# Layer 0's input projection on split operands for 18 of 20 tiles, the request part of the 31-tap convolution on GpSimd, and the first taps of the 4-tap convolution on ScalarE

## The reference, cut to what matters

```python
proj = h @ w_in                      # 640 x 1024 times 1024 x 2568
a_val, a_gate, z, xbc, dt_raw = split(proj, ...)     # 512, 512, 512, 1024, 8 columns
a_glu = a_val * sigmoid(a_gate)
a_conv = causal_dwconv(a_glu, conf_state, conf_w, conf_b)    # 31 taps, depthwise
a_out  = silu(layernorm(a_conv, ln_g, ln_b))
xbc_c  = silu(causal_dwconv(xbc, ssd_conv_state, xbc_w, xbc_b))  # 4 taps, depthwise
dt = softplus(dt_raw + dt_bias)
y  = ssd_scan(xs, dt, -exp(a_log), b_in, c_out, state)       # chunks of 64 frames
b_out = rmsnorm((y + d_skip * xs) * silu(z))
out = concat([a_out, b_out]) @ w_out
```

## Time and profile before

| what | value |
|---|---|
| time, median of 3 runs | 1737.92 us (1737.47 to 1738.1) |
| span of the profiled execution | 1735.7 us |
| between the two | 2.2 us |
| TensorE busy | 1702.0 us, 98% of the span |
| VectorE busy | 1058.7 us, 61% |
| ScalarE busy | 683.9 us, 39% |
| GpSimd busy | 370.5 us, 21% |
| stage of the change, on TensorE | 47.69 to 259.71 us |

### The profile page before, as it was taken

How to read it: one execution, slowest core, us unless ns; L and a number is a source line. 1 busy time by engine, 2 the same in 40 slices (tenths; PEclk the granted TensorE clock), 3 DMA queues, 4 the chain that set the end, 5 groups by cost and what they waited for, 6 DMA issues and landing times.

```text
span 1735.7 us, 27688 instructions
## 1 busy us (share of the span) xinstructions
PE 1702.0 (98%) x11360; PEld 1543.0 (89%) x11360; DVE 1058.7 (61%) x1717; ACT 683.9 (39%) x1219; POOL 370.5 (21%) x289
## 2 busy tenths in 40 slices
PE   7999998999999999999999999999999999999999
PEld 6566556797999999999989899789899999999999
DVE  3699867637667647465654424744676774655574
ACT  4111243435525525253552124633543453544352
POOL 3012100211104324132213132200110241414240
PEclk9999999999999999999999999999999999999999
DMA  8222330142303131403143221603320313122212
GB/s 263 101 77 103 93 107 28 49 195 98 104 27 138 32 130 46 135 19 128 31 141 74 75 73 64 246 27 114 153 93 25 128 48 115 61 70 86 87 66 91
DMA packets 39674, 162.30 MB, mean 94 GB/s; under 512 B 9384, under 2 KB 10280, under 8 KB 25600
## 3 DMA queue, kind: packets, MB, share of 16 engines
q1 hardware_dynamic: 32240, 124.59, 21.5%
q0 software_dynamic: 7312, 35.98, 5.8%
HBM read 149.87 MB, written 10.42 MB: 92 GB/s over the span
## 4 chain that ended last, share of the span: by engine, by line
PE 92%; DVE 5%; ACT 2%; issue 1%; DMA 0%; POOL 0%; SPq 0%; DVEq 0%; ACTq 0%
PE G L940 68%; PE S L940 11%; PE Q L940 11%; PE Q L1635 1%; ACT work L1731 0%; DVE rstd L2344 0%; DMA ring<-in_w_mk 0%; DVE ev_low L2593 0%; ACT rstd L1731 0%; DVE stats L2623 0%; DVE resid L2875 0%; ACT h_split L1731 0%; PE Q L1347 0%; DVE stats L2992 0%; DVE work L2636 0%
## 5 line engine op out<-in xcount | busy, mean ns | idle before, releaser
L940 PE MATMUL G<-ffn_rows,w_split 128*128 128x320 f32 x2160 | 329.8, 309 | 0.0
L940 PEld LDWEIGHTS G<-ffn_rows,w_split 128*128 128x128 f32 x2160 | 320.1, 188 | 0.0
L1731 ACT ACTIVATE w_split<-ring 128x512 fp32r<-128x512 f32 (+2 forms) x224 | 159.1, 711 | 316.8 <-PE G L940 208.4
L940 PE MATMUL G<-front,ring 128*128 128x128 f32 (+2 forms) x832 | 223.3, 430 | 11.0 <-DMA ring<-in_w_mk 9.3
L940 PEld LDWEIGHTS G<-front,ring 128*128 128x128 f32 x832 | 133.0, 193 | 100.0 <-issue 95.9
L856 POOL TENSOR_TENSOR mkT<-ring 128x512 f32<-128x512 f32 x72 | 98.2, 1369 | 564.6 <-DMA ring<-in_w_up 382.2
L940 PE MATMUL G<-h_split,w_split 128*128 128x320 f32 x1344 | 200.9, 310 | 1.2 <-DVE w_split L2359 0.8
L940 PEld LDWEIGHTS G<-h_split,w_split 128*128 128x128 f32 x1344 | 197.5, 188 | 1.9 <-issue 1.3
L940 PE MATMUL G<-g_split,w_split 128*128 128x320 f32 x1056 | 163.7, 310 | 0.1
L940 PEld LDWEIGHTS G<-g_split,w_split 128*128 128x128 f32 x1056 | 156.7, 188 | 1.7 <-DVE w_split L2848 1.4
L2715 DVE TENSOR_TENSOR w_split<-ring,w_split 128x512 fp32r<-128x512 f32 (+1 forms) x124 | 105.8, 854 | 59.9 <-ACT w_split L1731 58.7
(11 more groups left out here) (351 smaller groups left out, 2818.8 us busy)
## 6 DMA issues: line engine op xcount, KB each, us to landing
ring<-in_w_up SPq DMA_DIRECT2D x44, 1024.0 KB, 4.8
ring<-in_w_down SPq DMA_DIRECT2D x48, 256.0 KB, 2.6
ring<-in_w_down SPq DMA_DIRECT2D x32, 320.0 KB, 2.9
front<-in_mem_k POOLq DMA_DIRECT2D x8, 1024.0 KB, 6.1
front<-in_mem_v POOLq DMA_DIRECT2D x8, 1024.0 KB, 10.6
ring<-in_w_mk SPq DMA_DIRECT2D x4, 1024.0 KB, 5.9
ring<-in_w_mv SPq DMA_DIRECT2D x4, 1024.0 KB, 10.9
ring<-in_w_glu SPq DMA_DIRECT2D x4, 1024.0 KB, 8.6
```

Of the source, the lines that this page charges most:

```text
L940: return nc.tensor.matmul(out, lhsT, rhs, start=start, stop=stop, **kw)
L1731: return nc.scalar.activation(*a, **k)
```

## The change

The 20 input tiles of layer 0 are made in two ways. The first gate and value tile stay in f32 (`first_pair`), and the strips of `dtp` now stand between the steps of the gate tile. The other 18 tiles (6 `glu`, 8 `xbc`, 4 `z`, counted `i` = 0 to 17) are made by `input_product(i)` from split rows and split weights. ScalarE writes the high rows into the space of the residual `x` and the high weights into four (later two) slots; VectorE subtracts the low rows in place of the normalized rows `h` and the low weights in place of the loaded ones. Since `x` is overwritten, SP loads it again behind the last `z` tile.

The 31 taps of the 128 request columns go to GpSimd (`request_taps`): for each of four channel blocks one first tap, then 30 products and 30 additions. The 512-column taps stay on VectorE; each now waits for the one directly ahead of it, and the partial sums lie in PSUM (`S`), until the last tap writes SBUF. `memory_keys(1)` stands between the second and third block on GpSimd. The first tap of the 4-tap convolution moves to ScalarE (`xbc_first`). The sum of the four convolution results moves behind the first two blocks of the 4-tap convolution (`taps_sum`).

```diff
-for _n, _c in (("mk0", 4), ("mv0", 2), ("glu", 8), ("dtp", 1), ("mk1", 4), ("dt", 1), ("mv1", 2), ("xbc", 8),
+for _n, _c in (("mk0", 4), ("mv0", 2), ("dtp", 1), ("glu", 8), ("mk1", 4), ("dt", 1), ("mv1", 2), ("xbc", 8),
...
+            def input_product(i, halfway=None):
...
+                pe.wait_ge(in_split, i + 1)
+                weights = [in_piece(i)[1], in_piece(i)[2]]
+                for k in range(KD):
+                    if i == 0:
+                        pe.wait_ge(in_lo, k + 1)
+                    for wpart, xpart in ((0, 0), (0, 1), (1, 0)):
+                        for f in range(2):
+                            fr = slice(f * HT, (f + 1) * HT)
+                            m = mm(out[:, fr], weights[wpart][:, k, :], in_rows[xpart][:, k, fr],
...
-            projections("glu", 8, KD, rows(h), norm="mix0")
-            narrow(TILE0["dtp"], "wdt", h)
+            first_pair()
+            for i in range(IN_GLU):
+                input_product(i)
...
+            def request_taps(j):
...
+                nc.gpsimd.tensor_scalar(out, padded(aglu, j, 0, CPROMPT, CREQ, 0)[1], pr("cw", j * CW), pr("cb", j),
+                                        ALU.mult, ALU.add).then_inc(taps_made, 1)
+                product(1)
+                for w in range(1, CW):
+                    if w + 1 < CW:
+                        product(w + 1)
+                    pool.wait_ge(taps_made, base + 2 * w)
+                    nc.gpsimd.tensor_tensor(out, out, runs(tap_room[:, w % 3, :]), ALU.add).then_inc(taps_made, 1)
...
-                        dve.wait_ge(conv, at - 1)
-                        ins = v.scalar_tensor_tensor(out=out, in0=src, scalar=tap, in1=out,
-                                                     op0=ALU.mult, op1=ALU.add)
+                        dve.wait_ge(conv, at)
+                        ins = v.scalar_tensor_tensor(out=part if w < CW - 1 else acc[:, j, 0:SEQ], in0=src, scalar=tap,
+                                                     in1=part, op0=ALU.mult, op1=ALU.add)
...
+                if j == 0:
+                    input_low(2)
+                conv_taps(9)
+                if j in (1, 2):
+                    input_low(1)
+                conv_taps(8)
+            input_low(2)
             step_sizes()
-            conv_taps(8 * CW - taps_done[0])
+            conv_taps(14)
+            input_low(2)
+            conv_taps(27)
+            input_low(1)
+            conv_taps(8)
+            input_low(1)
+            conv_taps(4 * CW - taps_done[0])
...
+                if c == CHUNK["evout"] + 3:
+                    tile_wait(sp, z_tile(3))
+                    for k in range(0, KD, 2):
+                        sp.dma_start(x[:, k:k + 2, :], dram["x"][:, k:k + 2, :]).then_inc(x_again, 16)
```

More of the change, by code:

```diff
@@ new lines, in first_pair @@
+            def first_pair():
+                n = TILE0["glu"]
+                steps, gate, value = begin(n - 1), begin(n), G[(n + 1) % 2]
+                s = chunk(CHUNK["glu"])
+                pe.wait_ge(par_in, 16)
+                for k in range(KD):
+                    pe.wait_ge(applied, APPLIED["mix0"] - KD + 1 + k)
+                    q, o = k % 4, PAR["wdt"][0] + k * NH
+                    strip, w = slice(32 * q, 32 * q + 32), par[:, o:o + 32]
+                    mm(steps[strip, 0:512], w, h[:, k, 0:512], k < 4, k >= 4, tile_position=(0, 32 * q))
+                    m = mm(steps[strip, 512:T], w, h[:, k, 512:T], k < 4, k >= 4, tile_position=(0, 32 * q))
+                    if k == KD - 1:
+                        m.then_inc(tile_done, 1)
+                    w = ring[:, s, k * 256:k * 256 + P]
+                    mm(gate[:, 0:512], w, h[:, k, 0:512], k == 0, k == KD - 1)
+                    m = mm(gate[:, 512:T], w, h[:, k, 512:T], k == 0, k == KD - 1)
+                m.then_inc(tile_done, 1)
+                begin(n + 1)
+                for k in range(KD):
+                    w = ring[:, s, k * 256 + P:k * 256 + 2 * P]
+                    mm(value[:, 0:512], w, h[:, k, 0:512], k == 0, k == KD - 1)
+                    m = mm(value[:, 512:T], w, h[:, k, 512:T], k == 0, k == KD - 1)
+                    m.then_inc(h_used if k < KD - 1 else tile_done, 1)
@@ L1120, in _ @@
             memory_values(1)
[L1121 to L1125, removed]
+            for i in range(IN_GLU, IN_XBC):
+                input_product(i)
+                if i == IN_GLU + 5:
+                    conv_stat(3)
+            for i in range(IN_XBC, IN_XBC + 2):
+                input_product(i)
             nready[0] += 4
@@ L1138, in _ @@
                 .then_inc(tile_done, 1)
-            s = chunk(CHUNK["z"] + 1)
-            for n in range(2, 4):
-                project(z_tile(n), s, n % 2 * P, KD, rows(h), halfway=h_free if n == 3 else None)
+            for i in range(IN_XBC + 2, IN_TILES):
+                input_product(i, halfway=h_free if i == IN_TILES - 1 else None)
             RUN, CSK = NCH - 1, 64 + NH
@@ L1880, in _, with input_high @@
             memory_values(0, 1)
+            act.wait_ge(mem_key_eps, 4)
+            for k in range(KD):
+                act.wait_ge(applied, APPLIED["mix0"] - KD + 1 + k)
+                A(x_r[:, k, :], h[:, k, :], ACT.Copy).then_inc(in_hi, 1)
+            def input_high(i):
+                user = in_slot_user(i)
+                if user >= 0:
+                    tile_wait(act, in_tile(user))
+                src, hi, _ = in_piece(i)
+                name, at = ("glu", i + 2) if i < IN_GLU else ("xbc", i - IN_GLU) if i < IN_XBC else ("z", i - IN_XBC)
+                chunk_wait(act, CHUNK[name] + at // 2)
+                A(hi, src, ACT.Copy).then_inc(in_high, 1)
             t0 = TILE0["glu"]
+            input_high(0)
+            input_high(1)
+            act.wait_ge(par_in, 16)
+            evacuate(dt_parts, TILE0["dtp"])
             for j in range(4):
@@ L1884, in _ @@
                     read_wait(act, t0 + 2 * (j - 2) + 1)
-                evacuate(tmp[:, j % 2, :], t0 + 2 * j, ACT.Sigmoid)
-            act.wait_ge(par_in, 16)
-            evacuate(dt_parts, TILE0["dtp"])
-            log_exp_table()
-            memory(1)
+                tile_wait(act, t0 + 2 * j)
+                A(tmp[:, j % 2, :], glu_out(t0 + 2 * j), ACT.Sigmoid).then_inc(read[(t0 + 2 * j) % 2], 1)
+                if j < 2:
+                    input_high(2 + 2 * j)
+                    input_high(3 + 2 * j)
+            log_exp_table()
+            head_norms(lambda j: mkT[:, 1, j, :], TILE0["mk1"], 4, 1.0 / P, MT)
+            for m2 in range(2):
+                input_high(IN_GLU + 2 * m2)
+                input_high(IN_GLU + 2 * m2 + 1)
+                memory_values(1, m2)
             def xbc_rows(j):
@@ L1911, in _ @@
             act.wait_ge(applied, APPLIED["mem"])
-            for j in range(6):
+            act.wait_ge(pads_in, 16 * 12)
+            for j in range(4):
                 xbc_rows(j)
-            for j in range(2):
-                xbc_silu(j)
+                if j < 2:
+                    xbc_first(j)
+                input_high(IN_GLU + 4 + j)
+            xbc_silu(0)
+            xbc_rows(4)
+            xbc_silu(1)
+            xbc_rows(5)
             r = sums(1)
```

146 lines of the change are left out of this document (113 added, 33 removed).

## The result

The changed kernel takes 1742.99 us (median of 10 runs, 1741.89 to 1744.28), the kernel before 1737.88 in the same comparison: a ratio of 1.003, 95% interval 1.0021 to 1.0039. It is 5.1 us slower, where 6.3 us less were forecast, and it lies inside the stated range. The scan starts at 264.31 us instead of 259.71, 4.6 later, so most of the loss lies in the stage of the change. Behind the scan's start no wait of TensorE has grown up to the end of the output projection, but the rest of the changed kernel's span is 0.9 us longer (1476.9 against 1476.0).

The account below looks back on a forecast made before the run. TensorE was full with VectorE close behind, and VectorE was to become the bound. Tiles -28.6, strips +6.3 and stalls +16.3 gave -6.0, row by row -6.3: 1737.92 - 6.3 = 1731.6 us, range 1719 to 1750.

Parts of the forecast that it names:

- split tiles: TensorE's 18 split input tiles: 7.06 us each instead of 8.65, 28.6 us saved.
- VectorE became the bound: Input stage: VectorE gets 2.1 us more to do while TensorE gets 22.3 less, so VectorE becomes the bound.
- the large gaps: TensorE waits for VectorE: 6.3 us before tile 5, 5.0 us before the column sum behind the sixth `xbc` tile.
- dear PSUM taps: Rival, VectorE's 124 taps: above 0.78 us each through PSUM, up to 0.90 and 1743.6 us; chance 17%.
- a late GpSimd: Rival, request taps: GpSimd holds the sums from 0.89 us a pair; at 1.20, 1763 us; chance 19%.
- "I take the loss" of the strips: TensorE's gate tile and `dtp` strips: each strip streams alone, 17.3 us instead of 11.0, a loss of 6.3.
- The rival in which strips overlap: Gate tile: strips still overlap, 6.3 us less; part of "more is saved", 1724 to 1726 us, chance 18%.
- GpSimd "costs nothing up to 0.89": Request taps on GpSimd: 0.74 us a pair, two blocks end at 190.2, sums want them at 199.1; no cost.
- The clock as a rival: TensorE's clock falls in the stalls, 2.6 us lost each: 1734.2 us with one loss, 1736.8 with two; chance 18%.
- the gap ahead of tile 12: TensorE waits 2.8 us there for one more 4-tap convolution block and a low weight on VectorE.
- ScalarE at nothing: ScalarE's 18 weight and 8 row copies and first taps, some 45 us, cost nothing except before low weight 6.
- The reload of `x` and the state's load: Reload issued near 252, 21 us under cover until past 299; state's load near 200 instead of 207; no cost.

Follow-up runs that it names:

- Run 1: Changed kernel with the eight strip steps together again, ahead of the gate tile's last step: 1734.27 us, ratio 0.9979 to the kernel before.
- run 4: Changed kernel with strips in a block again and the low weights of tiles 4 and 5 made earlier: 1731.74 us, ratio 0.9963.
- Run 3: Changed kernel with GpSimd making only the first of the 31 request taps: 1738.87 us, ratio 1.0002 to the kernel before.
- Run 12: Changed kernel with unread matmuls in TensorE's waits: eight ahead of tile 5, nine ahead of the column sum, three ahead of tile 12: 1738.82 us.
- run 10: Changed kernel with unread matmuls in TensorE's waits: nine ahead of the column sum, three ahead of tile 12: 1741.06 us.
- run 2: Changed kernel with the low weights of tiles 4 and 5 right behind the second pair's multiplication: 1739.74 us, ratio 1.0009.
- run 7: Run 3's kernel with VectorE's partial sums in SBUF instead of PSUM: 1738.48 us against 1738.87.
- run 6: Run 4's kernel, last pair's multiplication earlier (1727.13 us), then also column sum behind xbc tile 7, low weights and ScalarE moves reordered: 1736.75 us.
- run 9: Run 6's kernel with ScalarE moving tiles 10 and 11 out earlier, three low weights earlier, squares' sums ahead of decay sums: 1724.81 us.
- run 8: Changed kernel with nine unread 512-column matmuls in TensorE's wait ahead of the column sum: 1743.02 us.

## Why the prediction was wrong, step by step

The forecast was a gain of 6.3 us, and a loss of 5.1 was measured: 11.4 us apart. The mechanism was right: split tiles save what was said (tiles 0 to 4 ran from 76.39 to 111.84, 7.09 each), VectorE became the bound, the large gaps stood at tile 5 and at the column sum, and the scan followed VectorE's chain (runs 1 and 4). Three terms of the sum were mis-sized, all to the same side. The prediction gave 27% to a slower kernel, all of it to dear PSUM taps and a late GpSimd; neither came, and the kernel was slower all the same. That the time lies inside the range, which a late GpSimd had widened to 1750, is luck.

- **"I take the loss" of the strips, 17.3 us for gate and strips.** Measured 19.5. A strip step and a whole-array step together cost 2.44 us, not 2 x 1.08: 2.2 us over the eight, and the stage began 0.5 later. Why the pair costs 0.28 more than two lone streams is open. Run 1 prices the whole interleave at 8.7 us of time, where the sum had 6.3. The rival in which strips overlap is refuted.
- **GpSimd "costs nothing up to 0.89".** The term asked only when GpSimd ends. It ended in time, though 14 us later than forecast, but its work lengthened VectorE's low weights and 4-tap blocks, which still have two SBUF inputs. The rows that said so were in hand (7.36 instead of 3.02 us) and were weighed for the taps alone. Run 3 prices it at 4.1 us.
- **The clock as a rival, not in the sum.** The gaps were forecast at 6.3 and 5.0 us, and a loss behind each was priced at 2.6, then left to a chance of 18%. Both losses came, at 1.6 and 1.3 us, and a third behind the 1.5 us gap ahead of tile 12. The 2.6 was read from a stretch whose granted clock is 1.00, so those rows don't show that it was a price of the clock. Run 12 prices them at 4.2 us with the 1.7 of tile 12; run 10 shows 1.9 of it for the late gaps. The Trainium skill (TensorE: Matmul & The Clock Gate, Part 1) says that an idle array falls back to half rate; the windows above agree, with a clock of 0.50 at 211.2 to 213.0.

Together 2.2 + 0.5 + 4.1 + 4.2 = 11.0 of the 11.4. The runs do not show that these four are strictly independent; runs 1, 2 and 4 only show that two other gains add, and no run undoes strips, taps and clock together. The rows of the account above divide the same loss otherwise: strips 2.2, start 0.5, gaps 3.0 longer than forecast, half rate 4.6, and 0.9 behind the scan, where the prediction had nothing. Smaller: a tap takes 0.79 instead of 0.78, which is 1.2 us over 124, and the gap ahead of tile 12 was 1.5 instead of 2.8.

- **PSUM taps.** The rival was refuted: 0.79 in either memory (run 7). The argument against it was weaker than it looked: all three rows read a PSUM buffer, so they compare no memory with another. The Trainium skill (Perfetto Trace Analysis, Optimizing Scalar/DVE Operations) gives VectorE about twice the access overhead on PSUM; these taps with two inputs show none of it, the first tap with one input shows 0.27 us.
- **ScalarE at nothing** held for its work and not for its order: what bound run 6, and in part run 9, was a move out of PSUM that stood in its queue behind a wait for VectorE.
- **The reload of `x` and the state's load** made no wait on TensorE longer, as said. The 0.9 us behind the scan lie in matmuls that run a little longer, and no run ties them to either load.

## What to carry to other kernels

When a change makes one engine faster and loads its neighbour, lay both queues out, and then add what each forecast gap costs beyond itself: here the gaps cost 19.3 us and half rate behind them another 4.2 of time. Ask of work moved to an idle engine not only whether it ends in time but which instructions of the others it makes longer. And before giving up such a change, look for what the waiting engine waits for: the order of the queues alone, with the same 28472 instructions, took this one from 5.1 us slower to 17.6 us faster.

## What the runs showed that was not expected

- Alternating 32-column strips with whole-array matmuls made a pair of steps 2.44 us, which leaves 1.36 for the strip if the whole-array step keeps its 1.08; strips in a block took 0.29. Not only the four at a time are lost, a quarter comes on top of a lone stream.
- A gap of 2.65 us in which TensorE waited for VectorE was followed by a granted clock of 0.73 in the first 2.3 us of the next tile and 0.50 in the 2 us after that (run 8).
- A multiplication with one input takes 0.81 us from SBUF to PSUM and 0.54 from SBUF to SBUF; with two inputs there is no difference.
